# Index scores in pairs of heads, the select's test in a PSUM bank, projections on two banks: one step of a hybrid decoder trunk on one core

## The chip, the cores and the metric

The kernel runs on one core of a Trainium2 chip. The metric is the device time of one launch in microseconds, median of several runs. TensorE (PE) multiplies matrices into the eight banks of PSUM, the vector engine (DVE) and the scalar engine (ACT) work on SBUF and PSUM, GpSimd (POOL) works on SBUF and issues DMAs, and SyncE (SP) issues DMAs.

## The reference, cut to what matters

Two layers run over 1024 prompt tokens and 8 x 4 sample tokens. A layer projects its normalised input, runs four mixers (A to D), adds the output projection and a SwiGLU feed-forward. The change touches the index scores and the top-k of mixer A and the projections:

```python
def indexer_scores(iq, iw, ik):
    dots = jnp.einsum('nthe,nse->nths', iq, ik).astype(F32) * IDX_DIM ** -0.5
    return jnp.einsum('nth,nths->nts', iw.astype(F32) * IDX_HEADS ** -0.5, jax.nn.relu(dots))
...
        sc = indexer_scores(iqb, iwb, ik)
        sc = jnp.where(key_pos[None, None, :] <= tpos[None, :, None], sc, NEG_BIG)
        val, idx = lax.top_k(sc, k_sel)
```

There are 4 index heads of 64 elements and `k_sel` is 256. All arithmetic is float32.

## The kernel before

Every engine has its own hand-written program, a loop over the two layers, and the order in it is the order of the code. Engines meet through counting semaphores. The profiled layers begin near 28 and 1670 us.

**Index scores of the prompt.** `score_prompt` on TensorE (L767 to L782) runs head by head (h = 0 to 3) over the query tiles i = 2 to 7 of 128 tokens each. Tile i has (i + 1) x 128 keys. Heads 0 and 2 lie on partitions 0 to 63 of `iq`, heads 1 and 3 on 64 to 127, so a head contracts over 64 rows of the array. A step u writes two PSUM banks, three steps are in flight. `score` on ACT (L1507 to L1528) applies the ReLU into one of two SBUF buffers, and `score` on DVE (L1904 to L1944) multiplies by the head's weight and adds into `scs[i - 2]` (L1925 for the first head, L1927 for the others). Behind the six tiles of each head DVE also makes two rows of `HnR`, the low part of the normalised input (L1933), with the weights of a projection waiting for `x_lo`. After this come the causal masks (L1938), and on TensorE `score_sample` (L784 to L804), which starts when all 24 ReLUs are done and ends in `ss_sum`, for which DVE waits before L1940.

**Select.** `select` on DVE finds for every query the 256th largest score by fixing the 32 bits of the threshold one after the other, first for the 32 sample tokens (one block of 32 x 2080), then for the six prompt tiles. A bit is `counts` (L1961: comparison with the candidate and a count, one instruction per block), `missed` (L1967: is the count under 256, times the bit's value, into `MISS`) and the update of the candidate (L1979). Each of these is followed by a drain. `MISS`, `CNT`, `CAND` and the table of bits are all in SBUF. After bit 2 of the prompt's round `sample_softmax` waits for `as_qk`, that is for TensorE's `mask` of the sample logits (L967), and after bit 5 for an exponential on ACT.

**Projections.** During the select TensorE runs `sample_a`: 22 steps of projections, each split in a high and a low part of weights and input (L896, L910), cut in 72 units of 24 or 48 matmuls. Unit u writes bank 5 + u mod 3 and starts when unit u - 3 is evicted (`un_ev`), which ACT does (L1477, L1490). Between the steps stand the sample's attention scores, its mask and its values. ACT makes the high part of the weights two steps ahead, GpSimd the low part by a subtraction with two SBUF inputs (`low_weights`, L537). When all units are evicted, TensorE goes on to `attend(0)` (L818 scores, L826 mask by the selection). DVE's part of it begins, tile by tile, with `chosen` (L1993 to L2002), which turns threshold and scores into a mask. The additions of L2049 wait for the scores of TensorE and stand behind `chosen`.

## Time and profile before

| | us |
|---|---|
| three runs | 3338.89, 3351.86, 3354.99 |
| median | 3351.86 |
| profiled execution, whole time | 3342.51 |
| its span in the trace | 3340.8 |

| engine | busy us | share of the span |
|---|---|---|
| PE matmul | 3148.7 | 94% |
| PE weight load | 2871.3 | 86% |
| DVE | 1912.7 | 57% |
| ACT | 583.1 | 17% |
| POOL | 418.6 | 13% |

The chain of work that ended last gives 66% of the span to TensorE and 28% to DVE. 15% of it is one line, L1961, the counting of the select. Busy shares are averages over stages with different limits. What counts for the change is read from the stretch between the first index score and the first attention unit of each layer, some 400 us twice.

### The profile page before, as it was taken

How to read it: one execution, taken by the hardware profiler on the slowest of the kernel's cores; microseconds unless marked ns; L12 is line 12 of the kernel's file. 1: busy time of each engine (PE TensorE's matmuls, PEld its weight loads, DVE VectorE, ACT ScalarE, POOL GpSimd, SP SyncE). 2: the span in 40 equal slices, each digit the busy share in tenths (PEclk: the TensorE clock that was granted, in tenths of full speed). 3: DMA queues.
4: the chain of work that ended last, by engine and by line, in shares of the span. 5: the costliest groups of instructions: out<-in, count | busy, mean ns of one | idle time of the engine just before them, and what ended most of it. 6: DMA issues, size and time to landing. Idle time of an engine off the chain costs nothing.

```text
span 3340.8 us, 55923 instructions
## 1 busy us (share of the span) xinstructions
PE 3148.7 (94%) x21728; PEld 2871.3 (86%) x21728; DVE 1912.7 (57%) x3457; ACT 583.1 (17%) x1067; POOL 418.6 (13%) x594
## 2 busy tenths in 40 slices
PE   7999988898999999999989999789999999999997
PEld 4599975767899999999966999558688999999997
DVE  3699997687533333333427999966966333333335
ACT  3322112143200000000123221122332000000001
POOL 4133410001000000000041542000000000000000
PEclk9899998799999999999999999897999999999999
DMA  8144434233111111111152443252411111111112
GB/s 273 45 134 133 145 130 175 77 121 108 35 51 39 51 40 50 51 38 51 34 159 64 150 141 119 96 207 80 139 65 38 42 51 49 42 49 38 51 45 97
DMA packets 121147, 292.36 MB, mean 88 GB/s; under 512 B 19445, under 2 KB 70790, under 8 KB 116918
## 3 DMA queue, kind: packets, MB, share of 16 engines
q1 hardware_dynamic: 71938, 129.61, 11.2%
q0 software_dynamic: 33088, 102.84, 9.6%
q10 hardware_dynamic: 15844, 56.12, 4.8%
q8 instruction: 186, 3.05, 0.4%
q14 instruction: 91, 0.75, 0.1%
HBM read 242.24 MB, written 50.74 MB: 88 GB/s over the span
## 4 chain that ended last, share of the span: by engine, by line
PE 66%; DVE 28%; issue 3%; ACT 2%; DVEq 1%; DMA 0%; ACTq 0%; SPq 0%; POOL 0%; POOLq 0%
DVE U L1961 15%; PE PS L1243 14%; PE PS L1241 14%; PE PS L1239 14%; PE PS L757 3%; PE PS L1129 2%; PE PS L1265 2%; PE PS L1267 2%; PE PS L1266 2%; DVE smu L1967 1%; DVE smu L1979 1%; PE PS L818 1%; PE PS L840 1%; DVE U L2066 1%; PE PS L1230 1%
## 5 line engine op out<-in xcount | busy, mean ns | idle before, releaser
L1961 DVE TENSOR_SCALAR_CACHE_REDUCE U<-U,smu 32x2080 bf16<-32x2080 f32 (+6 forms) x462 | 504.6, 1146 | 13.5 <-issue 1.8
L2368 DVE TENSOR_TENSOR U<-PS,U 128x352 f32<-128x352 f32 x132 | 69.2, 524 | 545.0 <-ACT U L1752 544.8
L1243 PE MATMUL PS<-HNHR,WSR 128*128 128x352 f32 x1920 | 346.3, 322 | 0.0
L1239 PE MATMUL PS<-HNHR,WHR 128*128 128x352 f32 x1920 | 345.3, 321 | 0.0
L1241 PE MATMUL PS<-HnR,WHR 128*128 128x352 f32 x1920 | 345.3, 321 | 0.0
L1243 PEld LDWEIGHTS PS<-HNHR,WSR 128*128 128x128 f32 x1920 | 314.4, 188 | 0.0
L1239 PEld LDWEIGHTS PS<-HNHR,WHR 128*128 128x128 f32 x1920 | 313.5, 188 | 0.0
L1241 PEld LDWEIGHTS PS<-HnR,WHR 128*128 128x128 f32 x1920 | 313.5, 188 | 0.0
L507 POOL DMA_DIRECT2D WS<-wjobs x176 | 94.1, 535 | 1718.7 <-PE PS L1243 1471.7
L1752 ACT ACTIVATE U<-PS 128x352 f32<-128x352 f32 x132 | 61.6, 467 | 1346.6 <-PE PS L1243 1346.6
L1873 DVE CAST WHR<-WS 128x1024 fp32r<-128x1024 f32 (+2 forms) x152 | 94.5, 622 | 295.0 <-DMA WS<-wjobs 294.8
L1241 PE MATMUL PS<-HDLR,WHR 128*128 128x352 f32 x1056 | 200.7, 323 | 0.0
L1243 PE MATMUL PS<-HDHR,WSR 128*128 128x352 f32 x1056 | 200.6, 322 | 0.0
L1239 PE MATMUL PS<-HDHR,WHR 128*128 128x352 f32 x1056 | 200.5, 322 | 0.0
L537 POOL TENSOR_TENSOR WSR<-WS,HNHR 128x1024 fp32r<-128x1024 f32 x50 | 121.9, 2445 | 470.1 <-ACT HNHR L1377 470.0
L1243 PEld LDWEIGHTS PS<-HDHR,WSR 128*128 128x128 f32 x1056 | 175.2, 189 | 0.0
L1241 PEld LDWEIGHTS PS<-HDLR,WHR 128*128 128x128 f32 x1056 | 175.1, 188 | 0.0
L1239 PEld LDWEIGHTS PS<-HDHR,WHR 128*128 128x128 f32 x1056 | 174.8, 188 | 0.0
L1875 DVE TENSOR_TENSOR WSR<-WS,WHR 128x1024 fp32r<-128x1024 f32 (+2 forms) x152 | 164.9, 1085 | 11.4
L896 PE MATMUL PS<-XHR,HNHR 128*128 128x352 f32 x912 | 166.8, 324 | 0.0
L896 PE MATMUL PS<-XHR,WSR 128*128 128x352 f32 x912 | 165.1, 323 | 0.0
L896 PE MATMUL PS<-HnR,HNHR 128*128 128x352 f32 x912 | 164.9, 322 | 0.0
(293 smaller groups left out, 4966.0 us busy)
## 6 DMA issues: line engine op xcount, KB each, us to landing
WS<-wjobs POOLq DMA_DIRECT2D x113, 512.0 KB, 3.9
WS<-wjobs ACTq DMA_DIRECT2D x50, 512.0 KB, 4.4
WS<-wjobs POOLq DMA_DIRECT2D x48, 384.0 KB, 3.4
Hn<-ckT SPq DMA_DIRECT2D x16, 896.0 KB, 9.9
U<-kT_pool SPq DMA_DIRECT2D x160, 64.0 KB, 2.1
xres<-U SPq DMA_DIRECT2D x2, 4224.0 KB, 15.3
U<-xres SPq DMA_DIRECT2D x4, 2112.0 KB, 7.6
U<-v_pool SPq DMA_DIRECT2D x128, 64.0 KB, 2.3
```

Source lines behind the costliest of these rows:

```text
L507: pool.dma_start(slot(j % NJOBS, n), wjobs[bass.ds(L * NJOBS + j, 1), :, 0:n].rearrange("a p n -> (a p) n")).then_inc(w_in[j % NJOBS % NSL ...
L537: pool.tensor_tensor(out=WSR[:, j % NSLOT, 0:1024], in0=slot(j, 1024), in1=high_weights(a).bitcast(F32), op=ALU.subtract).then_inc(wp_lo, 1)
L757: i = mm(PS[:, base + c, 0:CW], w[:, k, :], Hn[:, k, c * CW:(c + 1) * CW], start=k == 0, stop=k == KR - 1)
L896: m = mm(out, w[:, k * P:(k + 1) * P], x[:, k, t], start=n == 0 and k == 0, stop=n == 2 and k == KR - 1)
L1129: m = mm(blocks(PS[:, 2 * (s % 3) + a, i * n:(i + 1) * n], l), keys(l, a * 64, r)[:, t], queries(quer(l, a * 64, r)[:, t], l), start=True, ...
L1239: mm(out, w(k)[0], x(k)[0], start=k == 0, stop=False)
L1241: mm(out, w(k)[0], x(k)[1], start=False, stop=False)
L1243: i = mm(out, w(k)[1], x(k)[0], start=False, stop=k == n - 1)
L1873: v.tensor_copy(hi, x)
L1875: return tt(out=lo, in0=x, in1=hi.bitcast(F32), op=ALU.subtract)
L1961: ts(U[0:m, JUNK[i]:JUNK[i] + w // 2].bitcast(BF16), s, CANDF[0:m, i:i + 1], None, op, ALU.add, accum_out=into[0:m, i:i + 1])
L2368: tt(out=x, in0=PS[:, 2 * (t % 3) + 1, 0:CW], in1=U[:, SIL + (t % 3) * CW:SIL + (t % 3 + 1) * CW], op=ALU.mult)
```

## The change

It has three parts.

1. The index scores run over 12 pairs (r, i). The two heads of a pair lie on the two halves of the partitions, and their matmuls alternate, each pair of heads into four PSUM banks, with two pairs in flight. ACT and DVE take the heads of a pair one after the other. DVE adds a drain ahead of each second head. The eight L1933 operations leave the loop and stand behind the causal masks, ahead of the wait for `ss_sum`.
2. `MISS` moves from SBUF to columns 0 to 6 of PSUM bank 7, and `missed` becomes a `tensor_scalar` with the bit's value as a pointer scalar. The update reads `MISS` from PSUM and `CAND` from SBUF.
3. Projection units alternate between banks 5 and 6, and unit u waits for the eviction of unit u - 2.

```diff
--- before.py
+++ after.py
@@ -294,7 +294,7 @@
         LB, OML, EPSC = sm[:, 83:85], sm[:, 85:87], sm[:, 90:91]
         SMX, SRS, SRC = sm[:, 87:88], sm[:, 88:89], sm[:, 89:90]
         WSEL = sm[:, 96:128]
-        CAND, MISS = smu[:, 0:7], smu[:, 7:14]
+        CAND, MISS = smu[:, 0:7], PS[:, 7, 0:7].bitcast(U32)
         CANDF = CAND.bitcast(F32)
         NRM = ((nrm_sq, nrm_acc, nrm_sum, nrm_inv), (first_sq, first_acc, first_sum, first_inv),
                (first_sq, first_acc, first_sum, first_inv))
@@ -387,7 +387,7 @@
 
         def unit_bank(u):
 
-            return 5 + u % 3
+            return 5 + u % 2
 
         def high_weights(a):
 
@@ -402,6 +402,9 @@
             for q, a in enumerate(KEPT[i]):
                 sent[a] += 16 * (q + 1)
             at_ = (KEPT[i][-1] + 1) % 3
+
+
+        SCORED = [(r, i) for r in range(2) for i in range(2, TILES)]
 
         def job_bank(n):
 
@@ -767,19 +770,17 @@
             def score_prompt():
 
                 pe.wait_ge(pj_ev, 4 * len(PI))
-                u = 0
-                for h in range(H):
-                    a, r = (h % 2) * 64, h // 2
-                    for i in range(2, TILES):
-                        if u >= 3:
-                            pe.wait_ge(sc_relu, u - 2)
-                        b, n = 2 * (u % 3), (i + 1) * P
-                        for o in range(0, n, 512):
-                            w = min(512, n - o)
-                            m = mm(PS[:, b + o // 512, 0:w], iq[a:a + 64, r, i * P:(i + 1) * P],
-                                   iq[a:a + 64, 2, o:o + w], start=True, stop=True)
-                        m.then_inc(sc_ps, 1)
-                        u += 1
+                for q, (r, i) in enumerate(SCORED):
+                    if q >= 2:
+                        pe.wait_ge(sc_relu, 2 * (q - 1))
+                    n = (i + 1) * P
+                    for o in range(0, n, 512):
+                        w = min(512, n - o)
+                        for a in range(2):
+                            rows_ = slice(64 * a, 64 * a + 64)
+                            m = mm(PS[:, 4 * (q % 2) + 2 * a + o // 512, 0:w], iq[rows_, r, i * P:(i + 1) * P],
+                                   iq[rows_, 2, o:o + w], start=True, stop=True)
+                    m.then_inc(sc_ps, 1)
 
             def score_sample(L):
 
@@ -882,8 +883,8 @@
                 pe.wait_ge(wp_hi, max(SPLIT_NO[j] for j in jobs) + 1)
                 for c in units or range(UNIT[i + 1] - UNIT[i]):
                     u = UNIT[i] + c
-                    if u >= 3:
-                        pe.wait_ge(un_ev, u - 2)
+                    if u >= 2:
+                        pe.wait_ge(un_ev, u - 1)
                     if kind == "T":
                         hi, lo = high_weights(ats[0]), WSR[:, jobs[0] % NSLOT, 0:1024]
                         out, t = PS[:, unit_bank(u), 0:CW], part(c)
@@ -1505,17 +1506,16 @@
                                       ).then_inc(st_out[KEPT[i][1]], 16)
 
             def score(L):
-                u = 0
-                for h in range(H):
-                    for i in range(2, TILES):
-                        act.wait_ge(sc_ps, u + 1)
+                for q, (r, i) in enumerate(SCORED):
+                    act.wait_ge(sc_ps, q + 1)
+                    n = (i + 1) * P
+                    for a in range(2):
+                        u = 2 * q + a
                         if u >= 2:
                             act.wait_ge(sc_acc, u - 1)
-                        n = (i + 1) * P
-                        act.activation(U[:, RELU + (u % 2) * SEQ:RELU + (u % 2) * SEQ + n],
-                                       PSF[:, 1024 * (u % 3):1024 * (u % 3) + n], ACT.Relu, scale=E ** -0.5
+                        o = 2048 * (q % 2) + 1024 * a
+                        act.activation(U[:, RELU + a * SEQ:RELU + a * SEQ + n], PSF[:, o:o + n], ACT.Relu, scale=E ** -0.5
                                        ).then_inc(sc_relu, 1)
-                        u += 1
                 act.wait_ge(out_dma, 48)
                 for i in range(2):
                     high_part(L, i)
@@ -1914,28 +1914,28 @@
                     v.tensor_copy(WCOL[h * NS:(h + 1) * NS, :], WQ[0:NS, 8, h:h + 1])
                 v.drain()
                 ts(WSEL, cst(C_TOK, NS), WCOL, None, ALU.mult).then_inc(ss_wsel, 1)
-                u = 0
-                for h in range(H):
-                    for i in range(2, TILES):
-                        v.wait_ge(sc_relu, u + 1)
-                        n = (i + 1) * P
-                        r = U[:, RELU + (u % 2) * SEQ:RELU + (u % 2) * SEQ + n]
-                        w = WQ[:, i, h:h + 1]
-                        if h == 0:
-                            ts(scs[i - 2], r, w, None, ALU.mult).then_inc(sc_acc, 1)
-                        else:
-                            stt(out=scs[i - 2], in0=r, scalar=w, in1=scs[i - 2], op0=ALU.mult, op1=ALU.add
-                                ).then_inc(sc_acc, 1)
-                        u += 1
-                    if h == 0:
-                        v.wait_ge(x_hi, KR)
-                    for k in (2 * h, 2 * h + 1):
-                        tt(out=HnR[:, k, :], in0=Hn[:, k, :], in1=XHR[:, k, :].bitcast(F32), op=ALU.subtract
-                           ).then_inc(x_lo, 1)
-                    v.drain()
+                for q, (r, i) in enumerate(SCORED):
+                    if q == TILES - 2:
+                        v.drain()
+                    n = (i + 1) * P
+                    for a in range(2):
+                        v.wait_ge(sc_relu, 2 * q + a + 1)
+                        x, w = U[:, RELU + a * SEQ:RELU + a * SEQ + n], WQ[:, i, 2 * r + a:2 * r + a + 1]
+                        if r == 0 and a == 0:
+                            ts(scs[i - 2], x, w, None, ALU.mult).then_inc(sc_acc, 1)
+                            continue
+                        if a == 1:
+                            v.drain()
+                        stt(out=scs[i - 2], in0=x, scalar=w, in1=scs[i - 2], op0=ALU.mult, op1=ALU.add
+                            ).then_inc(sc_acc, 1)
+                v.drain()
                 for i in range(2, TILES):
                     d = scs[i - 2][:, i * P:(i + 1) * P]
                     tt(out=d, in0=d, in1=cst(C_TRI, P), op=ALU.add)
+                v.wait_ge(x_hi, KR)
+                for k in range(KR):
+                    tt(out=HnR[:, k, :], in0=Hn[:, k, :], in1=XHR[:, k, :].bitcast(F32), op=ALU.subtract
+                       ).then_inc(x_lo, 1)
                 v.wait_ge(ss_sum, 1)
                 v.tensor_copy(ss[:, 0:PAST], PSF[0:NS, 0:PAST])
                 tt(out=ss[:, PAST:SW], in0=PS[0:NS, 4, 0:NS], in1=CT[0:NS, C_SEQM:C_SEQM + NS], op=ALU.add)
@@ -1964,8 +1964,7 @@
 
                     def missed(b):
                         counts(ALU.is_ge, CNT)
-                        stt(out=MISS[:, c], in0=CNT[:, c], scalar=float(TOPK), in1=bc(cst(C_BITF + b, 1), 1, n)[:, :, 0],
-                            op0=ALU.is_lt, op1=ALU.mult)
+                        ts(MISS[:, c], CNT[:, c], float(TOPK), cst(C_BITF + b, 1), ALU.is_lt, ALU.mult)
                         v.drain()
 
                     missed(0)
```

TensorE, start of the index scores in a layer, rows before and after. `U` holds queries and keys, `PS` is PSUM, and xN counts equal neighbours.

```order
L779 MATMUL PS<-U 128x384
L779 MATMUL PS<-U 128x512 x2
L779 MATMUL PS<-U 128x128
L779 MATMUL PS<-U 128x512
L779 MATMUL PS<-U 128x256
L779 MATMUL PS<-U 128x512
```

```order
L781 MATMUL PS<-U 128x384 x2
L781 MATMUL PS<-U 128x512 x4
L781 MATMUL PS<-U 128x128 x2
L781 MATMUL PS<-U 128x512 x2
L781 MATMUL PS<-U 128x256 x2
L781 MATMUL PS<-U 128x512 x2
```

Every shape now stands twice in a row, once for each half of the partitions.

DVE, the middle of the scoring before and its second half after. L1933 before and L1937 after write `HnR`.

```order
L1925 TENSOR_SCALAR U<-U,sm 128x1024
L1933 TENSOR_TENSOR HnR<-Hn,XHR 128x1056 x2
L1927 SCALAR_TENSOR_TENSOR U<-U,sm 128x384
L1927 SCALAR_TENSOR_TENSOR U<-U,sm 128x512
L1927 SCALAR_TENSOR_TENSOR U<-U,sm 128x640
L1927 SCALAR_TENSOR_TENSOR U<-U,sm 128x768
L1927 SCALAR_TENSOR_TENSOR U<-U,sm 128x896
L1927 SCALAR_TENSOR_TENSOR U<-U,sm 128x1024
L1933 TENSOR_TENSOR HnR<-Hn,XHR 128x1056 x2
```

```order
L1925 TENSOR_SCALAR U<-U,sm 128x1024
L1929 SCALAR_TENSOR_TENSOR U<-U,sm 128x1024
L1929 SCALAR_TENSOR_TENSOR U<-U,sm 128x384 x2
L1929 SCALAR_TENSOR_TENSOR U<-U,sm 128x512 x2
L1929 SCALAR_TENSOR_TENSOR U<-U,sm 128x640 x2
L1929 SCALAR_TENSOR_TENSOR U<-U,sm 128x768 x2
L1929 SCALAR_TENSOR_TENSOR U<-U,sm 128x896 x2
L1929 SCALAR_TENSOR_TENSOR U<-U,sm 128x1024 x2
L1934 TENSOR_TENSOR U<-U,CT 128x128 x6
L1937 TENSOR_TENSOR HnR<-Hn,XHR 128x1056 x8
L1940 COPY U<-PS 32x2048
```

The eight rows of `HnR` that stood in twos between the heads stand together behind the causal masks, ahead of the copy that waits for `ss_sum`.

DVE, the first bits of the select for the sample. `sm` and `smu` are SBUF, `BITU` and `CT` are tables in SBUF.

```order
L1961 TENSOR_SCALAR U,sm<-U,smu 32x2080
L1967 SCALAR_TENSOR_TENSOR smu<-sm,CT 128x1
L1972 TENSOR_SCALAR smu<-smu 128x1
L1974 TENSOR_TENSOR smu<-smu,BITU 128x1
L1961 TENSOR_SCALAR U,sm<-U,smu 32x2080
L1967 SCALAR_TENSOR_TENSOR smu<-sm,CT 128x1
```

```order
L1961 TENSOR_SCALAR U,sm<-U,smu 32x2080
L1967 TENSOR_SCALAR PS<-sm,CT 128x1
L1971 TENSOR_SCALAR smu<-PS 128x1
L1973 TENSOR_TENSOR smu<-smu,BITU 128x1
L1961 TENSOR_SCALAR U,sm<-U,smu 32x2080
L1967 TENSOR_SCALAR PS<-sm,CT 128x1
L1978 SCALAR_TENSOR_TENSOR smu<-PS,BITU,smu 128x1
```

The test writes `PS` in place of `smu`, and what follows it reads `PS`. The number of instructions per bit stays the same.

## Rows read from the trace of the kernel before

**Rows 1.** Stretches of layer 0: us, busy PE PEld DVE ACT POOL, PEclk, DMA, GB/s.

```profile
117.00:130.00 13.00, 11.80 (x18) 5.14 (x17) 8.08 (x9) 4.79 (x7) 0.00 (x0) 0.50 0.00 0
480.00:530.00 50.00, 24.77 (x132) 13.02 (x132) 46.12 (x91) 9.42 (x29) 0.00 (x0) 0.71 0.35 128
```

**Rows 2.** Timeline (start, us, instruction, [idle before]): the end of the select, layer 0.

```profile
480.22 0.49 PE L818 MATMUL PS<-U 64*128 64x128 f32 x4 [0.47 <-ACT U L1377]
485.73 0.17 DVE L1986 TENSOR_SCALAR sm<-sm 128x6 f32<-128x6 f32 x1
489.49 0.29 DVE L2049 CUSTOM_DVE_ANT_0 U<-PS,U 128x128 f32<-128x128 f32 x1 [0.21 <-issue]
```

**Rows 3.** Timeline: two pairs of small operations of the select, and GpSimd.

```profile
162.28 0.16 DVE L1967 SCALAR_TENSOR_TENSOR smu<-sm,CT 128x1 uint32<-128x1 f32 x1
162.51 0.22 DVE L1979 SCALAR_TENSOR_TENSOR smu<-smu,BITU 128x1 uint32<-128x1 uint32 x1
165.28 1.63 DVE L1967 SCALAR_TENSOR_TENSOR smu<-sm,CT 128x1 uint32<-128x1 f32 x1
164.49 2.40 POOL L537 TENSOR_TENSOR WSR<-WS,HNHR 128x1024 fp32r<-128x1024 f32 x1 [28.15 <-ACT HNHR L1377]
```

**Rows 4.** Vector engine by line and shape, whole span: x, busy us, mean ns.

```profile
L1961 DVE TENSOR_SCALAR_CACHE_REDUCE U<-U,smu 128x1024 bf16<-128x1024 f32 x66 | 84.2, 1276 | 0.0
L1967 DVE SCALAR_TENSOR_TENSOR smu<-sm,CT 128x1 uint32<-128x1 f32 x64 | 24.9, 389 | 4.8
L1967 DVE SCALAR_TENSOR_TENSOR smu<-sm,CT 128x6 uint32<-128x6 f32 x64 | 23.9, 373 | 4.8
L1979 DVE SCALAR_TENSOR_TENSOR smu<-smu,BITU 128x1 uint32<-128x1 uint32 x60 | 23.7, 394 | 5.3 <-issue 0.9
L1979 DVE SCALAR_TENSOR_TENSOR smu<-smu,BITU 128x6 uint32<-128x6 uint32 x60 | 17.6, 294 | 4.5
L1938 DVE TENSOR_TENSOR U<-U,CT 128x128 f32<-128x128 f32 x12 | 2.6, 287 | 0.2
L2072 DVE TENSOR_TENSOR U<-PS,U 128x128 f32<-128x128 f32 x64 | 18.3, 286 | 13.5 <-ACT U L1377 13.1
...
L1925 DVE TENSOR_SCALAR U<-U,sm 128x384 f32<-128x384 f32 (+5 forms) x12 | 7.0, 587 | 9.5 <-ACT U L1515 9.4
L1927 DVE SCALAR_TENSOR_TENSOR U<-U,sm 128x384 f32<-128x384 f32 (+5 forms) x36 | 33.3, 950 | 8.1 <-ACT U L1515 6.9
```

**Rows 5.** Timeline: the mask on TensorE, and the select where it waits for it.

```profile
291.65 3.84 PE L967 MATMUL PS<-U,CT 48*128 48x512 f32 x10
297.26 2.32 DVE L2007 TENSOR_REDUCE sm<-PS 128x1 f32<-128x2080 f32 x1
```

**Rows 6.** Timeline of the scoring, layer 0 and, last two rows, layer 1.

```profile
91.90 8.08 PE L779 MATMUL PS<-U 64*128 64x384 f32 x24 [1.40 <-ACT U L1377]
94.25 1.75 ACT L1515 ACTIVATE U<-PS 128x384 f32<-128x384 f32 x3
105.29 4.38 DVE L1927 SCALAR_TENSOR_TENSOR U<-U,sm 128x640 f32<-128x640 f32 x4 [0.17 <-ACT U L1515]
129.62 5.28 PE L794 MATMUL PS<-U 128*128 128x512 f32 x8 [1.20 <-ACT U L1515]
1740.74 8.08 PE L779 MATMUL PS<-U 64*128 64x384 f32 x24 [1.40 <-ACT U L1377]
1775.10 5.16 PE L794 MATMUL PS<-U 128*128 128x512 f32 x8 [1.19 <-ACT U L1515]
```

**Rows 7.** Timeline: paired scores on TensorE in the attention.

```profile
501.05 1.68 PE L818 MATMUL PS<-U 64*128 64x512 f32 x4 [2.22 <-DVE sm L2049]
538.53 1.99 PE L818 MATMUL PS<-U 64*128 64x512 f32 x8
```

**Rows 8.** Timeline: the latest eviction of a projection, and the unit after next.

```profile
313.29 0.45 ACT L1490 ACTIVATE U<-PS 128x352 f32<-128x352 f32 x1
314.76 1.43 PE L896 MATMUL PS<-XHR,HNHR 128*128 128x352 f32 x8
```

## Prediction

> **What bounds the kernel now.** I read the chain of work that ended last first: in this stretch it runs over TensorE's index and sample scores, then over the select on DVE, then over the attention. So two questions decide: when do the index scores end, and what ends last behind them, the select or the projections that TensorE makes meanwhile.
>
> The end of the select is in [rows 2]. TensorE has finished its projections and starts the first attention scores at 480.22 (done at 480.71). DVE counts until 485.73, makes the mask of the first tile and comes to the first addition at 489.49. The select is late by 489.49 - 480.71 = 8.8 us. No more than that can be won in a layer by a faster select, since the projections are next. I take layer 1 as a repetition of layer 0.
>
> The scoring is in [rows 6]. It lasts from 91.90 to 129.62 = 37.7 us in layer 0, and from 1740.74 to 1775.10 = 34.4 us in layer 1; then the sample scores start, and behind them both the select and the projections. A microsecond won here moves both, so it counts in full. In layer 0 TensorE runs at half of its clock from 117 to 130 us (granted 0.50, the level of 1.2 GHz) [rows 1], after short idle gaps.
>
> **Part 1, the scoring.** TensorE is in the chain here because one head at a time uses half of the array's rows. The attention already pairs heads in this way. There a pair over 1024 keys, 8 instructions of 512 columns, takes 1.99 us, and a pair over 512 keys with the clock lower takes 1.68 us [rows 7]. Alone, the first 24 instructions, 427 columns each on average, take 8.08 us [rows 6], 0.79 ns a column against 1990 / (8 x 512) = 0.49 in the pair. The six tiles have 4224 keys. A round of six pairs then costs 1.99 x 4224 / 1024 = 8.2 us at the full clock and 1.68 x 4224 / 512 = 13.9 us at the lower one.
>
> DVE's own work per layer is 7.0 / 2 = 3.5 us of first products and 33.3 / 2 = 16.7 us of the others [rows 4], 20.2 us, running back to back as in the 4.38 us for four of them [rows 6]. The new drains ahead of each second head lay the end of one instruction before the start of the next. Between 162.28 + 0.16 and 162.51 this costs 0.07 us [rows 3], so 13 of them cost 1 us. ACT can't start before 94.25 - 91.90 = 2.35 us [rows 6], DVE follows 0.5 us later, and the last ReLU ends some 1.4 us ahead of DVE's end. With 1.6 us for handing over between the engines (my estimate, from the gaps of 0.17 and less in [rows 6]) the scoring takes 2.35 + 0.5 + 20.2 + 1 + 1.6 - 1.4 = 24.3, say 24.7 us at the full clock. Here DVE has become the limit. If the clock falls half way, the second round is TensorE's: 13.9 us in place of DVE's 16.7 x 2 / 3 = 11.1, with less overlap at its start, 28 us in all. If it is low from the start, two rounds of 13.9 and the rest give 32 us. I take 28, since TensorE now idles in every pair while DVE works, and idling like that came with a clock of 0.71 from 480 to 530 us, TensorE busy for 24.77 of 50 us [rows 1]. The gain is 37.7 - 28 = 9.7 in layer 0 and 34.4 - 28 = 6.4 in layer 1, less 0.2 for the last handover in each: **15.7 us**.
>
> The eight HnR operations move behind the masks. They cost nothing: they need some 10 us, up to 15 with GpSimd's subtraction beside them, and in that time TensorE is in its sample scores, which DVE waits for anyway. If this cover were gone, the select would start those microseconds later.
>
> **Part 2, the test in PSUM.** In [rows 3] the same test takes 0.16 us, and 1.63 us when GpSimd's subtraction runs from 164.49 to 166.89: DVE's ends at 166.91, with it. A small operation with two SBUF inputs is held until GpSimd is through. L1961, one SBUF input and a pointer scalar, is never held: its 66 instructions over 1024 columns average 1276 ns [rows 4], and holds of up to 2.4 us would show. After the change neither the test nor the update has two SBUF tensor inputs. Held time over the whole span, from 0.16 and 0.22 as undisturbed: in the prompt's rounds 23.9 - 64 x 0.16 = 13.7 and 17.6 - 60 x 0.22 = 4.4, so 9.0 us per layer; in the sample's rounds 24.9 - 10.2 = 14.7 and 23.7 - 13.2 = 10.5, so 12.6 us per layer [rows 4].
>
> The sample's 12.6 us are not won. After bit 2 of the prompt's rounds DVE needs TensorE's mask, ready at 291.65 + 3.84 = 295.49, and before it came there at 297.26 [rows 5]. It now comes some 12 us sooner and waits, so 1.8 us remain. The select thus ends 1.8 + 9.0 = 10.8 us sooner, plus what the new forms cost. The test gets a pointer scalar as the update has, 0.22 against 0.16 [rows 3]: 0.06 us a bit, 29 bits behind the mask, 1.7 us. A write of DVE into PSUM stands in no row. Below, a read costs nothing more: 286 ns from PSUM against 287 from SBUF over 128 columns [rows 4]. Above, neither form should cost more than the 0.286 us of those 128 columns, which adds 0.13 and 0.07, so 0.2 us a bit and 5.8 us a layer. I take 0.06, since the read is the nearest row. DVE then gains 9.1 and TensorE allows 8.8: **17.6 us** in two layers. At the upper price it is 5.0 a layer, 10.0 us. With the price under zero it stays 17.6.
>
> The Trainium skill ("VectorE: DVE Perf Modes", the section on the trn2 errata) gives an operation out of PSUM 62 cycles more of fixed cost than one within SBUF, which I estimate at 0.065 us. [Rows 4] show no such difference (286 against 287 ns). With that price on both instructions the select would gain 5.3 us a layer and not 8.8, and the time would be 7 us above my forecast.
>
> **Part 3, two banks.** TensorE starts a unit when the one before the last is evicted. The tightest place is behind the sample's exponential on ACT: an eviction ends at 313.29 + 0.45 = 313.74, and the unit that would wait for it starts at 314.76 [rows 8], 1.0 us later. So this costs nothing. Its cover is ACT being idle most of the time. If ACT came over 1.0 us later there, TensorE would stall by the excess, in two places a layer.
>
> **The sum.** 15.7 + 17.6 = 33.3 us off the profiled execution of 3342.5, so 3309. That execution is 9 us under the median of 3351.9, at which the forecast is made: 3351.9 - 33.3 = **3319 us**.
>
> **The rivals.**
> - The clock stays full during the scoring. Layer 1 had it longer than layer 0 (34.4 against 37.7 us). 24.7 us each give 13.0 + 9.7 = 22.7 and with the select 40 us: 3312. Against it stands the idling. 16%.
> - The clock is low all through: 32 us, a gain of 5.7 + 2.4 = 8 and 17.6: 3326. 8%.
> - The change doesn't do what it says, and DVE is still held. The cause may be any small operation beside GpSimd, not its two inputs. Then the scoring alone gains 15.7, and 0.06 us for 62 bits a layer is lost, 7.4: 3344. L1961 speaks against it. 9%.
> - The pairs don't overlap in this form. TensorE needs as much as before, and the time lies between 3327 and 3353, in the middle 3340. The attention speaks against it. 5%.
> - **Slower: PSUM costs the small operations much more.** Place: test and update, 33 bits ahead of the mask and 29 behind it. The margin at the mask eats 0.38 us a bit (12.6 / 33). Above that a bit costs in full: the sum of both layers is -2 x 10.8 + 58x - 15.7 up to the margin, and -2 x 10.8 - 25.2 + 124x - 15.7 beyond. It is zero at x = 0.5 us a bit, three times what the two take now in addition. At 0.65 it is +18 us: 3370. From 0.1 to 0.5 it lies between 3320 and 3352. For it: no row shows DVE writing PSUM, and every one of these operations is followed by a drain. Against it: the read row. 10%, of which 4 from 0.63 on.
>
> **How the numbers follow.** The forecast has 52%. "Faster by over 0.5%" is under 3335, which is about what a measurement of this kernel can tell, its three runs lying 0.5% apart. The forecast, both clock cases and the mild end of the PSUM case are there: 75%. The held case, the unpaired case and the middle of the PSUM case are within 0.5%: 21%. Slower is 4%. The range reaches up to the held case, 3344, and down to the full clock less half of the spread of the runs, 3304; it leaves out the costly PSUM case and little else.
>
> **What would show it.** Scoring: from the first to the last L781 and on to the sample scores some 28 us, the HnR operations inside the sample scores. Select: the test at 0.22 us, no instruction of L1967 or L1978 over 0.3 us beside GpSimd; a wait of DVE for the mask of some 12 us; at the first addition of the attention DVE and TensorE less than 1 us apart. Two banks: no wait of TensorE for ACT in the projections. I am wrong if the test takes 0.4 us or more, if it is still held, or if the projections end later in relation to the sample scores.

## The result, and the profile after

The changed kernel takes 3305.19 us (median of 4 runs, 3300.76 to 3308.85) beside 3345.43 us for the kernel before (4 runs, 3338.89 to 3354.99): a ratio of 0.9876, 95% interval 0.985 to 0.9902. It is faster by 1.2%. The gain is 40 us; the sum had 33.3. The time lies at the low end of the range of 3304 to 3344, where the rival "the clock stays full" stands with its 40 us.

The chain of work that ended last, first by engine and then by line (shares of the span):

```profile
span 3305.0 us, 55905 instructions
PE 74%; DVE 19%; issue 3%; ACT 2%; DVEq 1%; DMA 0%; ACTq 0%; SPq 0%; POOL 0%; POOLq 0%
PE PS L1244 14%; PE PS L1242 14%; PE PS L1240 14%; DVE U L1961 10%; PE PS L897 6%; PE PS L760 3%; PE PS L1130 2%; PE PS L1266 2%; PE PS L1268 2%; PE PS L1267 2%; PE PS L911 2%; PE PS L819 1%; PE PS L841 1%; PE PS L860 1%; DVE U L2048 1%
```

Before, DVE had 28% of this chain and TensorE 66%, and the projections (L897, before L896) were not among the lines that its page lists; the counts of the select (L1961) had 15%. The select still stands in the chain, but from the mask to its end only.

**The scoring.** Stretches (us, busy PE PEld DVE ACT POOL, PEclk, DMA share, GB/s) of the kernel after, two of layer 0 and the whole scoring of each layer, then the timeline of its scoring's start, of a pair over 1024 keys in layer 1, and of the ends in both layers:

```profile
105.00:117.00 12.00, 8.80 (x36) 3.67 (x36) 10.38 (x12) 8.29 (x13) 0.00 (x0) 0.86 0.00 0
117.00:130.00 13.00, 12.16 (x33) 5.91 (x34) 12.81 (x13) 2.59 (x3) 5.06 (x2) 1.00 0.00 0
...
92.73:117.84 25.11, 18.16 (x81) 7.42 (x81) 19.89 (x30) 20.16 (x35) 0.00 (x0) 0.93 0.18 54
1725.61:1749.86 24.25, 17.16 (x81) 6.80 (x81) 19.93 (x30) 20.26 (x35) 1.37 (x3) 1.00 0.51 141
```

```profile
92.73 1.77 PE L781 MATMUL PS<-U 64*128 64x384 f32 x8 [1.40 <-ACT U L1378]
...
117.84 3.69 PE L795 MATMUL PS<-U 128*128 128x512 f32 x8 [2.73 <-ACT U L1517]
...
124.67 8.26 DVE L1937 TENSOR_TENSOR HnR<-Hn,XHR 128x1056 fp32r<-128x1056 f32 x7
...
1744.21 7.03 DVE L1929 SCALAR_TENSOR_TENSOR U<-U,sm 128x768 f32<-128x768 f32 x6
1745.15 1.99 PE L781 MATMUL PS<-U 64*128 64x512 f32 x8 [0.19 <-ACT U L1517]
1749.86 2.41 PE L795 MATMUL PS<-U 128*128 128x512 f32 x5 [2.72 <-ACT U L1517]
```

The first stretch lies in the scoring, the second, but for its first 0.84 us, in the sample scores behind it. The granted clock is 0.86 and 1.00 in them, where it was 0.50 from 117 to 130 us before [rows 1]; over the whole scoring it is 0.93 in layer 0 and 1.00 in layer 1, with TensorE busy for 18.16 of 25.11 and 17.16 of 24.25 us. The scoring goes from 92.73 to 117.84 = 25.1 us in layer 0 and from 1725.61 to 1749.86 = 24.2 us in layer 1, against 37.7 and 34.4 before [rows 6]. In its last part DVE runs six instructions back to back in 7.03 us while TensorE, done with its last pair at 1747.14, waits until 1749.86: 2.72 us idle. DVE sets the length, as the working for the full clock had it (24.7 us). The sample scores behind it, which began at half of the clock before (5.28 us for the first eight in layer 0 [rows 6]), run at the full clock in this execution: 3.69 us. That is not a property of the change: in another execution of the same kernel (the one run again below) they took 6.73 us in layer 1.

```profile
1749.37 6.73 PE L795 MATMUL PS<-U 128*128 128x512 f32 x8 [2.73 <-ACT U L1517]
```

**The select.** DVE by line and shape (x, busy us, mean ns | idle before), and the timeline at the mask and at the end of the select, layer 0 of the kernel after:

```profile
L1967 DVE TENSOR_SCALAR PS<-sm,CT 128x6 uint32<-128x6 f32 x64 | 14.5, 227 | 5.0
L1967 DVE TENSOR_SCALAR PS<-sm,CT 128x1 uint32<-128x1 f32 x64 | 14.2, 222 | 5.0
L1978 DVE SCALAR_TENSOR_TENSOR smu<-PS,BITU,smu 128x6 uint32<-128x6 uint32 x60 | 13.5, 224 | 5.2 <-issue 0.9
L1978 DVE SCALAR_TENSOR_TENSOR smu<-PS,BITU,smu 128x1 uint32<-128x1 uint32 x60 | 13.1, 218 | 5.0 <-issue 0.7
```

```profile
278.27 3.84 PE L968 MATMUL PS<-U,CT 48*128 48x512 f32 x10
...
282.14 2.32 DVE L2006 TENSOR_REDUCE sm<-PS 128x1 f32<-128x2080 f32 x1 [7.91 <-PE PS L968]
...
466.01 0.49 PE L819 MATMUL PS<-U 64*128 64x128 f32 x4 [0.47 <-ACT U L1378]
...
468.31 0.29 DVE L2048 CUSTOM_DVE_ANT_0 U<-PS,U 128x128 f32<-128x128 f32 x1 [0.21 <-issue]
```

The test and the update take 0.22 to 0.23 us in each of the four groups, where they averaged 0.29 to 0.39 [rows 4]: none is held. DVE stands before the mask for 7.91 us. At the end of the select TensorE's first attention scores are done at 466.50 and DVE's first addition comes at 468.31, 1.8 us late in place of 8.8 [rows 2]. So the select gained 7.0 us in layer 0; in layer 1 the distance from the start of the scores to the addition went from 9.57 to 2.33 us, 7.2.

**Where the 35.8 us of span went** (3340.8 to 3305.0; start to start, layer 0 and layer 1):

| stretch | before | after | gain |
|---|---|---|---|
| index scores | 37.7, 34.4 | 25.1, 24.2 | 22.7 |
| sample scores to attention scores | 350.6, 350.2 | 348.2, 348.2 | 4.4 |
| attention scores to first addition | 9.3, 9.6 | 2.3, 2.3 | 14.2 |
| first addition to output projection | 306.0, 313.3 | 312.1, 311.5 | -4.3 |
| the rest | | | -1.3 |

The gains are taken from the unrounded times. The fourth line has nothing that the change touched. Over the traces of all kernels here it lies between 304.5 and 313.3 us, and the execution of before had one of its shortest.

### The profile page after: what moved, and what is told of

Its sections match the earlier page's. It is cut to its first block, busy times and chain, and to the rows that moved or that the text cites. A ratio compares the mean times of both kernels' runs of the same rounds, so it can differ in the third digit from the quotient of the medians.

```text
span 3305.0 us, 55905 instructions
## 1 busy us (share of the span) xinstructions
PE 3113.3 (94%) x21712; PEld 2856.1 (86%) x21728; DVE 1881.2 (57%) x3457; ACT 581.5 (18%) x1067; POOL 419.2 (13%) x594
## 4 chain that ended last, share of the span: by engine, by line
PE 74%; DVE 19%; issue 3%; ACT 2%; DVEq 1%; DMA 0%; ACTq 0%; SPq 0%; POOL 0%; POOLq 0%
PE PS L1244 14%; PE PS L1242 14%; PE PS L1240 14%; DVE U L1961 10%; PE PS L897 6%; PE PS L760 3%; PE PS L1130 2%; PE PS L1266 2%; PE PS L1268 2%; PE PS L1267 2%; PE PS L911 2%; PE PS L819 1%; PE PS L841 1%; PE PS L860 1%; DVE U L2048 1%
## 5 line engine op out<-in xcount | busy, mean ns | idle before, releaser
L1961 DVE TENSOR_SCALAR_CACHE_REDUCE U<-U,smu 32x2080 bf16<-32x2080 f32 (+6 forms) x462 | 504.7, 1146 | 12.6 <-issue 0.7
L1875 DVE TENSOR_TENSOR WSR<-WS,WHR 128x1024 fp32r<-128x1024 f32 (+2 forms) x152 | 164.9, 1085 | 12.1 <-issue 0.9
L897 PE MATMUL PS<-XHR,HNHR 128*128 128x352 f32 x912 | 166.8, 324 | 0.0
L897 PE MATMUL PS<-XHR,WSR 128*128 128x352 f32 x912 | 165.1, 323 | 0.0
L897 PE MATMUL PS<-HnR,HNHR 128*128 128x352 f32 x912 | 164.9, 322 | 0.0
```

Of the source, the lines that this page charges most:

```text
L897: m = mm(out, w[:, k * P:(k + 1) * P], x[:, k, t], start=n == 0 and k == 0, stop=n == 2 and k == KR - 1)
L1875: return tt(out=lo, in0=x, in1=hi.bitcast(F32), op=ALU.subtract)
L1961: ts(U[0:m, JUNK[i]:JUNK[i] + w // 2].bitcast(BF16), s, CANDF[0:m, i:i + 1], None, op, ALU.add, accum_out=into[0:m, i:i + 1])
```

## The experiments

The kernel before ran beside them and had medians of 3352.55 us (18 runs), 3349.78 us (12) and 3350.87 us (9) in the three groups. From the traces I read the length of the scoring in layers 0 and 1, the mean granted clock in it, and the distance from the start of the first attention scores to the first addition.

### Each part alone

Part 1 on the kernel before (pairs, both heads' banks and ReLUs, the HnR operations behind the masks; test, update and the three banks of the projections as before):

```diff
-                for h in range(H):
-                    a, r = (h % 2) * 64, h // 2
-                    for i in range(2, TILES):
+                for q, (r, i) in enumerate(SCORED):
+                    if q >= 2:
+                        pe.wait_ge(sc_relu, 2 * (q - 1))
...
```

> Kernel before plus part 1 (scores in pairs, HnR operations moved); test in SBUF and three banks as before. Theory A (the parts add up, and the scoring gains because TensorE's clock stays full): scoring 25 us in layer 0 and 24 in layer 1 against 37.7 and 34.4, sample scores 1.5 us shorter each, together some 26 us of the changed kernel's 36 in the profile; the small operations are held beside GpSimd as before, and the select ends 8 to 9 us after the projections. Time about 3319 where before is 3345. Theory B (the clock falls in this kernel, and full clock came from something else): scoring 28 us or more, gain 16 us.

Measured: 3321.62 us (3318.03 to 3323.57), ratio 0.9911 [0.9896, 0.9925]. Scoring 24.2 and 24.2 us at a clock of 0.99 and 1.00; scores to addition 9.6 us, and the tests still held (445 and 374 ns in the mean). Part 1 alone gives the whole length that the scoring has in the changed kernel. One thing of theory A did not come: the first eight sample scores were shorter in layer 1 only (3.69 us) and took 6.77 us in layer 0.

Parts 2 and 3 on the kernel before (test into PSUM, two banks for projections; heads one after the other):

```diff
-        CAND, MISS = smu[:, 0:7], smu[:, 7:14]
+        CAND, MISS = smu[:, 0:7], PS[:, 7, 0:7].bitcast(U32)
...
-            return 5 + u % 3
+            return 5 + u % 2
```

> Kernel before plus parts 2 and 3 (test into PSUM bank 7, two banks for projections); scoring as before. Theory A: scoring 37.7 and 34.4 us as before, no held small operation, DVE waits 6 to 8 us for the mask, first addition of the attention 2 to 2.5 us after TensorE's first scores in place of 9.3 and 9.6, a gain of 14 us: 3331 where before is 3345. Rival: with the old scoring the gain is another one, because the select starts against other GpSimd work; then not 2 to 2.5 us but more.

Measured: 3325.33 us (3320.4 to 3330.15), ratio 0.9925 [0.991, 0.994]. Scoring 33.5 and 34.6 us (clock 0.97, 0.94); scores to addition 2.0 us in both layers, so 7.4 us a layer won there; test and update at 0.22 us. The trace shows 15 us of gain in the select; the medians differ by 27. Some of the rest is the clock: the mean granted clock over the whole program was 0.9615 in the mean of these six runs, and 0.957 in the mean of the 18 runs of before beside them. Among all 39 runs of before in the three groups the time falls by some 2.1 us for 0.001 of clock, so about 9 of the 12 us go with it (an estimate from these runs). Why the clock was higher is not shown.

Part 3 alone:

```diff
-            return 5 + u % 3
+            return 5 + u % 2
...
-                    if u >= 3:
-                        pe.wait_ge(un_ev, u - 2)
+                    if u >= 2:
+                        pe.wait_ge(un_ev, u - 1)
```

> Kernel before with projections on two banks alone. Theory A: no wait of TensorE for ACT in the 72 units, projections from first to last as long as before (329.4 and 329.1 us), time same as before within 3 us. Rival: ACT comes over 1 us late in places, TensorE stalls, projections 2 us or more longer.

Measured: 3351.52 us (3340.45 to 3362.24, 10 runs), ratio 0.9995 [0.9982, 1.0007]: no difference. The projections take 328.6 us from first to last in both layers, against 328.9 and 328.7 before. They wait for no eviction: the list of TensorE's waits has none with the projections' line. But its profiled execution took 3362.24 us, and the scoring shows why; stretches of this kernel in layer 0 and layer 1:

```profile
92.00:105.00 13.00, 11.96 (x24) 5.81 (x23) 3.59 (x10) 6.38 (x17) 0.00 (x0) 0.61 0.33 103
...
117.00:130.00 13.00, 11.15 (x22) 5.20 (x23) 10.63 (x13) 6.78 (x9) 0.00 (x0) 0.67 0.00 0
...
1760.00:1775.00 15.00, 13.30 (x26) 6.53 (x24) 8.11 (x9) 5.08 (x8) 0.00 (x0) 0.55 0.13 38
```

The scoring, whose code is that of before, took 41.5 and 47.9 us, with a mean clock of 0.73 and 0.60.

Only the HnR operations moved behind the masks, heads one after the other:

```diff
-                    if h == 0:
-                        v.wait_ge(x_hi, KR)
-                    for k in (2 * h, 2 * h + 1):
-                        tt(out=HnR[:, k, :], in0=Hn[:, k, :], in1=XHR[:, k, :].bitcast(F32), op=ALU.subtract
-                           ).then_inc(x_lo, 1)
...
+                v.wait_ge(x_hi, KR)
+                for k in range(KR):
+                    tt(out=HnR[:, k, :], in0=Hn[:, k, :], in1=XHR[:, k, :].bitcast(F32), op=ALU.subtract
+                       ).then_inc(x_lo, 1)
```

> Kernel before with only the eight HnR operations moved behind the masks; the heads one after the other on three bank pairs. Theory A: with the 2.4 us pauses gone TensorE sets the pace, 80 instructions at 0.36 us, scoring 31 us in both layers, a gain of 6.7 and 3.4, so about 10 us: 3335. Rival 1: pairing was needed for any gain, scoring stays at 34 us or more. Rival 2: moving alone gives all, scoring 25 us.

Measured: 3339.91 us (3331.88 to 3347.83), ratio 0.9958 [0.9933, 0.9983]. A stretch of each of its two scorings:

```profile
105.00:117.00 12.00, 10.60 (x36) 5.35 (x35) 9.24 (x10) 6.94 (x11) 0.00 (x0) 1.00 0.00 0
...
1760.00:1775.00 15.00, 13.23 (x21) 5.07 (x17) 6.21 (x7) 5.05 (x7) 0.00 (x0) 0.50 0.00 0
```

29.8 us in layer 0 at the full clock, 42.9 us in layer 1 at a mean of 0.65: one code, one execution. Theory A had 31 us in both; it holds where the clock is full. So at the full clock pairs are worth 29.8 - 24.2 = 5.6 us a layer over single heads with the same cover. The scoring of before was never seen at the full clock. From the five of its scorings at a clock of 0.94 and more (next section) I estimate 32.4 us there (length times clock), so moving the HnR operations is worth 2.6 us a layer. Together that is 8.2 us a layer or 16.4 of the 22.7 us; the other 6.3 are the lower clock in the profiled execution of before, less what a lower clock cost the changed one.

### How long the scoring of before takes

> The kernel before once more, unchanged, to see how long its scoring takes in another execution: 37.7 and 34.4 us at a granted clock of 0.82 and 0.94 in the one the prediction was made from. Theory (its length goes by the clock of TensorE, which is another each time): some other pair of lengths between 30 and 48 us, longer where the clock is lower, and everything else as it was. Rival: 37 and 34 us again.

The kernel before once more gave 3346.06 us with a scoring of 34.5 and 33.6 us (clock 0.94 and 0.96). With this, ten scorings with single heads are known. These are the eight whose code is that of before, in order of their clock:

| mean clock in the scoring | 0.60 | 0.73 | 0.82 | 0.94 | 0.96 | 0.97 |
|---|---|---|---|---|---|---|
| length, us | 47.9 | 41.5 | 37.7 | 34.4, 34.5, 34.6 | 33.6 | 33.5 |

Length times clock lies between 28.7 and 32.4 in all of them, and is 32.4 in the five with the highest clock: TensorE sets most of the length. With pairs, nine traces gave eighteen scorings. Without the two of the kernel with one pair in flight, sixteen are left: eleven took 24.2 to 24.3 us at a clock of 0.99 or 1.00, and five took 25.1 us at 0.92 or 0.93. So the clock falls with pairs too, but for a shorter time, and it costs 0.9 us and not 10, since DVE sets the length. In five of the sixteen (two of them the same) the clock was low at the start of the sample scores, whose first eight instructions then took 5.3 to 6.8 us in place of 3.7; with single heads that was so in nine of ten. The medians fit: the runs of the kernel before spread over 23 us (3342.89 to 3366.04 in the first group), those of the changed kernel over 8.

### One pair in flight

The matmuls of a pair wait for both ReLUs of the pair before:

```diff
-                    if q >= 2:
-                        pe.wait_ge(sc_relu, 2 * (q - 1))
+                    if q >= 1:
+                        pe.wait_ge(sc_relu, 2 * q)
```

> The changed kernel with one pair in flight in place of two: a pair's matmuls wait until both ReLUs of the pair before have read their banks, so that TensorE stands idle in the scoring while ScalarE and VectorE work. The question is what pairing itself gives, and what the clock does. Theory A (matmuls of a pair and the ReLUs add up, the clock stays): scoring 33 us in place of 24.2 to 25.1, 8 to 9 us a layer, about 3322, granted clock in it above 0.9. Theory B (an idle TensorE loses its clock, which is why the scoring of the kernel before, with its half-used TensorE, varied from 29.8 to 47.9 us): the clock falls to 0.5 to 0.8 in it, and the scoring takes 40 to 50 us: 3335 to 3355.

Measured: 3354.89 us (3348.93 to 3358.75, 10 runs), ratio 1.0006 [0.9988, 1.0024], and so about 50 us above the changed kernel. Scoring 47.0 and 50.4 us. Two stretches and pieces of its timeline:

```profile
105.00:117.00 12.00, 8.07 (x22) 2.58 (x18) 3.48 (x4) 3.68 (x5) 0.00 (x0) 0.50 0.00 1
...
130.00:139.80 9.80, 4.31 (x20) 1.37 (x16) 5.29 (x5) 5.24 (x7) 0.00 (x0) 0.97 0.00 0
```

```profile
107.55 3.36 PE L781 MATMUL PS<-U 64*128 64x512 f32 x8 [1.62 <-ACT U L1517]
...
110.95 1.73 ACT L1517 ACTIVATE U<-PS 128x896 f32<-128x896 f32 x2 [3.46 <-PE PS L781]
...
132.16 1.77 PE L781 MATMUL PS<-U 64*128 64x512 f32 x8 [1.61 <-ACT U L1517]
```

The forecast of theory B came out. A pair over 896 keys takes 3.36 us at a granted 0.50, in place of 1.77 at the full clock later in the same scoring (at 132.16); the ReLUs wait 3.46 us for it and TensorE 1.62 us for them. So the fear of the prediction, that TensorE loses its clock when it idles between pairs, fits these two scorings (mean clocks of 0.67 and 0.56). That idling alone decides is not shown: from 130 to 139.8 us of the same scoring TensorE was busy for 4.31 of 9.80 us at a clock of 0.97, and single heads had 0.50 at 13.23 of 15. Pairing is no gain by itself: with one pair in flight the scoring (47.0 and 50.4 us) is longer than nine of the ten with single heads, and that eats what the select, untouched at 2.3 us, wins.

### The order of a pair's matmuls

```diff
-                    for o in range(0, n, 512):
-                        w = min(512, n - o)
-                        for a in range(2):
+                    for a in range(2):
+                        for o in range(0, n, 512):
+                            w = min(512, n - o)
...
```

> The changed kernel with the same pairs in flight and the same banks, but the matmuls of one head all issued before those of the other, in place of alternating between the two halves of TensorE's rows. Theory A (the gain comes from the two heads' matmuls lying over each other, which needs them to alternate): a pair's matmuls take up to twice as long, TensorE is again the bound of the scoring, its length goes by the clock as in the kernel before, 30 to 48 us a layer in place of 24 to 25: 3320 to 3345. Rival B (TensorE lets them overlap only where one head's last matmul meets the other's first, and having two heads of banks in flight is what counts): 25 to 28 us, 3307 to 3312.

Measured: 3304.29 us (3303.17 to 3304.99), ratio 0.9857 [0.9835, 0.9879], the changed kernel's time. Scoring 24.3 us in both layers. Its timeline of a pair over 1024 keys:

```profile
111.45 1.99 PE L781 MATMUL PS<-U 64*128 64x512 f32 x8 [0.18 <-ACT U L1517]
```

Eight instructions in 1.99 us, as with alternation. The records of the single instructions start in twos, 0.013 us apart (0.006 with alternation). One head's four can't follow each other so closely, so I read the second of each two as the other head's, though all of the first head's were issued ahead of it. Both theories gave a longer scoring, so both fall: with up to four instructions a head, the order within a pair does not matter.

### What holds a small operation

The changed kernel with MISS in SBUF, in the new form of the test:

```diff
-        CAND, MISS = smu[:, 0:7], PS[:, 7, 0:7].bitcast(U32)
+        CAND, MISS = smu[:, 0:7], smu[:, 7:14]
```

> The changed kernel with MISS back in SBUF and everything else kept: the test is still the tensor_scalar form (count, K, bit from a constant column), but its result lies in SBUF, so the update reads two SBUF tensors again. Theory A (what is held is an operation with two tensor inputs in SBUF, while GpSimd works): the test stays near 0.22 us, since it has one tensor input; the update goes back to 0.29 to 0.39 us in the mean, with single ones of over 1 us beside GpSimd's operations. In the kernel before, the updates' own holds were about a third of all; in one round they would be some 60 updates by 0.07 to 0.17 us in the whole select, of which the part behind TensorE's mask counts, 29 bits a layer by about 0.12 us = 3.5 us a layer, 7 us: about 3312. Rival B (the bank of its own matters, not the number of inputs): the test from SBUF to SBUF is held as well, 0.37 us in the mean, the select is as late as before (from the last attention scores to the first addition 9 to 10 us), 14 to 15 us lost: about 3320. Rival C (the form alone was the matter): neither is held, 3305.

Measured: 3320.39 us (3318.8 to 3321.41), ratio 0.9921 [0.9902, 0.994]; scores to addition 9.9 us, 7.6 a layer more than with the bank. The groups, and two places of the timeline with GpSimd beside it:

```profile
L1967 DVE TENSOR_SCALAR smu<-sm,CT 128x6 uint32<-128x6 f32 x64 | 28.9, 451 | 5.0
L1978 DVE SCALAR_TENSOR_TENSOR smu<-smu,BITU 128x1 uint32<-128x1 uint32 x60 | 28.7, 479 | 5.0 <-issue 0.7
L1978 DVE SCALAR_TENSOR_TENSOR smu<-smu,BITU 128x6 uint32<-128x6 uint32 x60 | 17.7, 295 | 5.2 <-issue 0.9
L1967 DVE TENSOR_SCALAR smu<-sm,CT 128x1 uint32<-128x1 f32 x64 | 13.7, 214 | 5.0
```

```profile
184.64 2.39 POOL L540 TENSOR_TENSOR WSR<-WS,HNHR 128x1024 fp32r<-128x1024 f32 x1 [9.97 <-ACT HNHR L1378]
...
186.40 0.21 DVE L1967 TENSOR_SCALAR smu<-sm,CT 128x1 uint32<-128x1 f32 x1
...
430.42 4.76 POOL L540 TENSOR_TENSOR WSR<-WS,HNHR 128x1024 fp32r<-128x1024 f32 x2 [9.53 <-ACT HNHR L1378]
...
432.95 2.25 DVE L1967 TENSOR_SCALAR smu<-sm,CT 128x6 uint32<-128x6 f32 x1
```

The test reads one tensor and a pointer scalar, and over six columns it is held all the same: 2.25 us, until GpSimd's second operation ends at 435.18. Over one column it is not: ten such tests ran inside a subtraction of GpSimd, the one at 186.40 among them, and took 212 to 215 ns. Over six columns twelve started inside one, and all were held. The update with two SBUF inputs is held in both shapes. So the sentence of the prediction, "neither the test nor the update has two SBUF tensor inputs", describes only half of it. What is held beside GpSimd is the operation with two tensor inputs in SBUF, and also this one-input operation from SBUF to SBUF over six columns. With the output in PSUM 22 tests of the changed kernel started inside a subtraction, and none took over 228 ns. Theory A was right on the update and wrong on the test, rival B right on the six columns and wrong on the one; the time went by rival B, since the six-column rounds are those behind the mask. It is not every one-input operation from SBUF to SBUF either: L1961, which also counts, was not held over 1024 columns (1276 ns in the mean [rows 4]).

The Trainium skill draws a line that fits. "SBUF — State Buffer" (on the shared port pair) has an exclusive lock between GpSimd and a DVE operation that has two SBUF inputs or runs in a two-port mode. "VectorE: DVE Perf Modes" (the mode 2×_2P) gives that mode to one-input operations from SBUF to SBUF whose outermost dimension that is not one is even, or odd and the same on both sides. Six columns meet this, and the trace agrees with 451 ns in the mean. A single column has no such dimension, of which the page says nothing; here it behaves as without the mode (214 ns). With the output in PSUM there is no such mode, and the 227 ns agree. No run here asked for the mode itself, so that cause is argued from the three shapes and not shown.

### What a bit is worth, and the mask

The same test twice in each bit:

```diff
+                        ts(MISS[:, c], CNT[:, c], float(TOPK), cst(C_BITF + b, 1), ALU.is_lt, ALU.mult)
+                        v.drain()
```

> The changed kernel with a drain and the same test a second time in each bit of the search: about 0.30 us more a bit (0.22 the operation, the rest the drain), nothing else. It measures how much slack VectorE's chain has at the first attention addition. Theory: none, since VectorE is the late one there by 1.8 us in the changed kernel. Then every microsecond of the chain is a microsecond of the kernel: 29 bits behind the mask by 0.30 = 8.7 us a layer; the 22 or so bits ahead of it first use up the 7.9 us that VectorE waits for the mask. From the last attention scores to the first addition 2.3 becomes 11 us; about 17.4 us in the two layers, 3322 to 3326. Rival: TensorE's order hides part of it, since work behind the select fills in: 3310 or less.

Measured: 3325.31 us (3324.75 to 3328.29), ratio 0.994 [0.9921, 0.996]; scores to addition 12.1 and 12.2 us, 9.8 a layer more. The timeline of the kernel, at the mask and at its first addition:

```profile
283.23 2.33 DVE L2008 TENSOR_REDUCE sm<-PS 128x1 f32<-128x2080 f32 x1
...
478.19 0.29 DVE L2050 CUSTOM_DVE_ANT_0 U<-PS,U 128x128 f32<-128x128 f32 x1 [0.22 <-issue]
```

Counted from the start of the sample scores (116.14 us here), the first addition comes after 362.1 us in place of 350.5, 11.6 us a layer more. 29 bits by 0.30 us are 8.7. The 35 bits ahead of the mask cost another 10.5, of which DVE's wait of 7.9 us covers all but 2.6; DVE is 2.8 us later at the mask. TensorE's attention scores themselves come 1.7 us later (349.9 us from the sample scores in place of 348.2), and therefore the distance to the addition shows 9.8 only. So there is no slack behind the mask in the changed kernel, and 7.9 us of it ahead: what DVE loses behind the mask, the kernel loses.

The mask two bits later, the wait for the exponentials one bit later:

```diff
-                    if b == 2:
+                    if b == 4:
                         v.wait_ge(as_qk, 1)
...
-                    elif b == 5:
+                    elif b == 6:
                         v.wait_ge(as_exp, 1)
```

> The changed kernel with VectorE's mask evictions and exponentials' wait placed two bits and one bit later in the search (behind bit 4 and bit 6 in place of 2 and 5). In the changed kernel VectorE stands 7.9 us before the mask and is then 1.8 us late at the first attention addition. Theory: with more bits ahead of the mask that wait shrinks by the length of these bits and the end of the select moves forward by as much, until TensorE's last attention scores set the end: from these to the first addition 0.5 to 0.7 us in place of 2.3, about 1.7 us a layer, 3.4 us in all: about 3302. Rival: the masked scores come later, TensorE stands in wait of its bank, and the same time or more is lost: 3305 to 3315.

Measured: 3299.83 us (3297.23 to 3305.47), ratio 0.9863 [0.984, 0.9886]. Its timeline at the mask and at the first addition:

```profile
284.55 2.32 DVE L2006 TENSOR_REDUCE sm<-PS 128x1 f32<-128x2080 f32 x1
...
464.24 0.49 PE L819 MATMUL PS<-U 64*128 64x128 f32 x4 [0.47 <-ACT U L1378]
...
464.90 0.29 DVE L2048 CUSTOM_DVE_ANT_0 U<-PS,U 128x128 f32<-128x128 f32 x1 [6.37 <-PE PS L819]
```

DVE no longer waits at the mask, and at the end of the select it is 6.37 us early: now it waits for TensorE, 0.66 us after whose start the addition comes, in place of 2.30. TensorE's own way from the sample scores to the attention scores is as long as before in layer 0, 348.2 us. I ran it again beside the changed kernel:

> The changed kernel once more, unchanged, beside the version with the later mask: 3301 to 3309, a median of 3305; its scoring again 24 to 26 us in both layers, since VectorE sets its length and not TensorE.

> The changed kernel with the mask two bits and the exponentials' wait one bit later in the search, once more, in more rounds beside the changed kernel itself. Theory: 3.4 us below it (1.7 us a layer at the first attention addition), 3300 to 3302. Rival: the first comparison was chance, and the two agree within 1 us.

Measured: the changed kernel 3303.43 us (3300.75 to 3306.06, 4 runs; scoring 25.1 and 25.1), the later mask 3300.43 us (3299.28 to 3307.65, 5 runs). That is 3.0 us between the medians, and 1.6 us a layer in the traces (0.7 against 2.3 us from scores to addition, both layers, both runs). The ratios to the kernel before, 0.9853 and 0.985, do not separate the two; the trace does at the place of the edit, and for the whole time the gain of 3 us is likely and not shown. Of both it is the version to keep.

## Why the prediction was right or wrong

**What bounds the kernel: right.** The two questions, the end of the scoring and what ends last behind it, are where the time went: 22.7 and 14.2 of the 35.8 us of span.

**Part 1, the pairs: the mechanism right, the size too small, and this is the step that failed.** DVE's work of 20.2 us, its drains and the ends around it gave 24.7 us for the full clock, and the trace has 24.2 and 25.1. The step was "If the clock falls half way ... 28 us in all ... I take 28". I took it from the stretch of 480 to 530 us, where TensorE was busy for half of the time at a clock of 0.71 [rows 1]. In the scoring of the changed kernel it is busy for 18.16 of 25.11 us in layer 0 and 17.16 of 24.25 in layer 1, and the clock is 0.93 and 1.00. It does fall in layer 0, but too briefly to make TensorE the limit of a round; that costs 0.9 us there, where the working had 3.3. The term was 15.7 us and measured 22.7. The rival that had it, the full clock with 22.7, got 16%. With one pair in flight the clock does fall to 0.50 and the scoring takes 47 to 50 us, so such a loss exists; the mistake was to take it from a stretch with more idling, because I had no row of one with as little. Part of the 22.7 is the scoring that it was measured against: 6.3 us of it are the lower clock in that execution of before.

**What the clock does outside of the scoring: missed.** From the sample scores to the attention scores the two layers gained 4.4 us in all, which stood in no term. 3.1 of it are the first sample scores at the full clock (3.69 us in place of 5.28 and 5.16), and this is chance: five of the sixteen scorings with pairs have it otherwise, up to 6.77 us. The other 1.4 are the projections, which go with the pace of the select (328.1 us from first to last in place of 328.9 and 328.7; 328.1 with parts 2 and 3 alone, and 329.9 with the test twice in each bit).

**The sum: partly luck.** Its 33.3 us are near the 35.8 of the spans because part 1 was 7.0 too small and part 2 3.4 too large, and because the stretches without a term nearly cancel (+4.4, -4.3, -1.3).

**The base.** The forecast was laid on the median of 3351.9 of three runs. The kernel's other medians, 3350 to 3353, agree with it; only the four runs beside the changed kernel had 3345.43. The gain by medians is 40 us there and 47 (3350.87 - 3303.43) in the last group. The gain depends on which scoring of before one compares with, 33.6 to 37.7 us a layer in its two profiles and up to 47.9 with the same scoring in another kernel; I read a single execution's 37.7 and 34.4 as the kernel's length.

**The HnR operations cost nothing: right.** They lie inside the sample scores (124.67 on), 1.25 us each in place of 1.79. The six masks ahead of them are held beside GpSimd (5.44 us for six, 0.29 each before [rows 4]); the sample scores cover that too.

**Part 2, nothing is held: right.** No operation of L1967 or L1978 is held, each costs 0.22 to 0.23 us, and my 0.06 us a bit was right: an undisturbed bit takes 5.99 us in place of 5.93 for the prompt and 3.06 in place of 3.00 for the sample. It takes 5.99 and 3.06 with MISS in SBUF too, so the write into PSUM has no price of its own. The trace decides against the 62 cycles that I had cited from the Trainium skill ("VectorE: DVE Perf Modes", the trn2 errata): the update reading PSUM takes 0.22 us, as the one reading SBUF did undisturbed [rows 3].

**Part 2, the size: 14.2 us in place of 17.6.** The step that was off is "DVE then gains 9.1 and TensorE allows 8.8". Behind the mask the held time of before was 8.1 us in layer 0 and not 9.0 (test 10.87 - 29 x 0.167 = 6.0, update 8.39 - 28 x 0.226 = 2.1), and the new form gave back 29 x 0.06 = 1.7. That makes 6.4, and DVE gained 6.1 there; with the 1.7 of lateness at the mask it is 7.8. TensorE came 0.8 us sooner by itself, from the mask to its attention scores. That leaves 7.0, with DVE 1.8 us late. "Less than 1 us apart" was wrong. The wait for the mask was 7.91 us and not some 12: the forecast of it left out two things that its own rows had, the 1.8 us of lateness and the new form ahead of the mask, 35 x 0.06 = 2.1. The holds of 12.6 less both are 8.7.

**Part 3, two banks: right.** Nothing, 0.9995 [0.9982, 1.0007], and no wait in the projections. That the three banks made room for the test's bank is what they were given up for, and it cost nothing.

**The rivals.** PSUM at 0.5 us a bit and more: no, 0.06. Still held: not in the changed form, but the run with MISS in SBUF shows that the form without the bank gives 3320 us. Pairs that don't overlap: no. A low clock all through: no, 0.92 to 1.00 with two pairs in flight.

**What stays open.** Part 1 alone gives 31 us of median and parts 2 and 3 give 27, together 58, while both at once give 47. The traces add up (the scoring of 24.2, the select of 7.4 a layer); the medians don't. Most of the excess goes with a higher clock in the runs of parts 2 and 3 alone. What raises or lowers TensorE's clock from one execution to the next is open, and so is why the scoring with single heads can have 0.50 or 1.00 at the same busy share.

## What to carry to other kernels

Where TensorE works in short bursts between other engines' steps, compare its time at both clocks before trusting one profile: here the same code took 33.5 to 47.9 us. Part of a change's value can be that another engine, whose time does not vary, becomes the limit: 16.4 of the 22.7 us would be there at the full clock too, and the rest was 6.3 against this execution of before and would be more against a slower one. Keep a second piece of work in flight when shortening such bursts: with one pair the gain was zero. And look for small operations that end together with a GpSimd operation: putting the result in PSUM freed them for 0.06 us a bit, where changing their inputs alone did not.

## What the runs showed of the hardware

- A stretch of single-head scores, TensorE busy for some 90% of it with half of the rows, was granted anything from 0.50 (13.23 of 15 us busy) to 1.00 (10.60 of 12) for the same code in one execution. With pairs a scoring had 0.92 to 1.00 at some 70% busy (18.16 of 25.11 us, 17.16 of 24.25), and with one pair in flight a stretch had 0.50 at 8.07 of 12 us busy and a later one 0.97 at 4.31 of 9.80.
- Two heads' matmuls on different halves of the rows lie over each other even where one head's four instructions are all issued first: the eight take 1.99 us and start in twos, 0.013 us apart.
- A one-input DVE operation from SBUF to SBUF beside a GpSimd subtraction was held for up to 2.25 us over six columns (all 12 that started inside one) and not over one (10 inside, 212 to 215 ns). With its output in PSUM it was held in neither shape (227 and 222 ns).
- An operation of 128x128 with two SBUF inputs was held as well: the causal masks took up to 2.43 us beside a GpSimd subtraction, 0.28 us undisturbed.
